# Four column-group chains for the compression products of a two-block transformer kernel, and a padded gather tile

## The reference, cut to what matters

```
hid = silu(einsum('td,edf->tef', t, w1)) * einsum('td,edf->tef', t, w3)
y = einsum('tef,efd->td', hid * combine[..., None], w2)
```

```
hid   = gelu((window + cmp_pe) @ cmp_w1[x])      # x = 0 keys, 1 values; 2048 -> 256
k_cmp, v_cmp = hid @ cmp_w2[x]                   # 256 -> 64
```

## Time and profile before

| | |
|---|---|
| median of three runs | 2472.61 us |
| the profiled execution: its time, its span | 2475.7 us, 2473.9 us |
| TensorE matmul busy | 2269.3 us, 92% of the span |
| VectorE, ScalarE, GpSimd busy | 837.0, 513.2, 53.9 us |
| mean granted TensorE clock | 0.953 of full speed |
| gather products L1320, 768 records | 149.4 us busy |
| compression products L2096, 128 records | 28.4 us busy |

### The profile page before, as it was taken

One profiled execution on the slowest core, in us unless ns is written; L12 is line 12 of the kernel. 1 busy time (PEld: TensorE's weight loads), 2 busy tenths in 40 slices (PEclk: granted clock), 3 DMA queues, 4 the chain that ended last, 5 costly groups with the idle time before them and its releaser, 6 DMA issues. The chain is left out here.

```text
span 2473.9 us, 33836 instructions
## 1 busy us (share of the span) xinstructions
PE 2269.3 (92%) x12870; PEld 1724.1 (70%) x12870; DVE 837.0 (34%) x1877; ACT 513.2 (21%) x1174; POOL 53.9 (2%) x28
## 2 busy tenths in 40 slices
PE   8998899886999889988699999999999999999999
PEld 6766766543876766544575777888877677788887
DVE  3465233232456324223335333211122532321112
ACT  2213320002312331000333422010012243201000
POOL 0120000000021000000000000000000000000000
PEclk9889889998988998999899999999999999999999
DMA  7220249996321063999654134333345403343433
GB/s 228 80 87 35 103 170 378 425 425 240 113 87 44 35 272 146 419 425 420 224 136 145 35 137 136 137 137 136 136 159 137 145 34 137 102 140 135 168 136 119
DMA packets 165171, 426.67 MB, mean 172 GB/s; under 512 B 40409, under 2 KB 54294, under 8 KB 140454
## 3 DMA queue, kind: packets, MB, share of 16 engines
q1 hardware_dynamic: 165030, 424.80, 46.6%
HBM read 419.06 MB, written 1.05 MB: 170 GB/s over the span
## 5 line engine op out<-in xcount | busy, mean ns | idle before, releaser
L2061 PE MATMUL bank<-hT,W 128*128 128x256 f32 (+1 forms) x1440 | 329.5, 385 | 6.9 <-ACT b_gates L2189 5.9
L2061 PEld LDWEIGHTS bank<-hT,W 128*128 128x128 f32 (+1 forms) x1440 | 269.4, 190 | 53.0 <-issue 12.3
L261 PE MATMUL bank<-hT,W 128*128 128x272 f32 x928 | 247.6, 427 | 16.8 <-issue 11.7
L261 PEld LDWEIGHTS bank<-hT,W 128*128 128x128 f32 x928 | 191.3, 209 | 65.9 <-issue 23.3
L3038 PE MATMUL bank<-hT,W 128*128 128x256 f32 x1024 | 225.5, 381 | 6.7 <-DVEq L3095 6.7
L3054 PE MATMUL bank<-u_hid,W 128*128 128x256 f32 x1024 | 223.3, 379 | 0.0
L3038 PEld LDWEIGHTS bank<-hT,W 128*128 128x128 f32 x1024 | 195.6, 191 | 34.3 <-issue 7.4
L3054 PEld LDWEIGHTS bank<-u_hid,W 128*128 128x128 f32 x1024 | 194.6, 190 | 26.5
L1320 PE MATMUL bank<-e_sel,rowsH 128*128 128x128 f32 (+1 forms) x768 | 149.4, 328 | 0.0
L1434 PE MATMUL bank<-W,e_hs 128*32 128x256 f32 x1792 | 112.3, 409 | 32.3 <-DMA W<-in_w 29.8
L1320 PEld LDWEIGHTS bank<-e_sel,rowsH 128*128 128x128 f32 (+1 forms) x768 | 113.9, 204 | 37.2 <-issue 11.6
(11 more groups left out here) (555 smaller groups left out, 2784.4 us busy)
## 6 DMA issues: line engine op xcount, KB each, us to landing
W<-in_w SPq DMA_DIRECT2D x112, 1024.0 KB, 16.7
W<-in_w_in SPq DMA_DIRECT2D x41, 2048.0 KB, 8.1
e_Wd<-in_w SPq DMA_DIRECT2D x64, 1024.0 KB, 12.6
W<-in_w_up SPq DMA_DIRECT2D x16, 2048.0 KB, 8.4
W<-in_w_down SPq DMA_DIRECT2D x16, 2048.0 KB, 7.9
W<-in_w_out SPq DMA_DIRECT2D x8, 2048.0 KB, 8.2
e_w_ahead<-in_w SPq DMA_DIRECT2D x16, 1024.0 KB, 15.9
W<-in_mem_w_kv SPq DMA_DIRECT2D x6, 2048.0 KB, 10.3
```

The source lines that it names most:

```text
L261: mm = nc.tensor.matmul(bank[:, 0:T], w[:, k, c0:c0 + P], m.hT[:, k, :], **st)
L2061: mm = nc.tensor.matmul(o[0:n, 0:S2], w[:, k, a:a + n], m.hT[:, k, :], start=(k == 0), stop=(k == KT - 1))
```

## The change

**Gather.** `rowsH`'s first tile (16 tokens) is set to zero in all 128 rows by GpSimd at the start of `mix_and_route`; ScalarE waits for that before it copies the rows in; and the three products of a feature tile all take 128 rows.

**Compression.** The two chains of 16 become four chains of 8 in four column groups (keys first half, keys second half, values first half, values second half), issued alternately into partitions 0, 32, 64 and 96 of one bank, after both halves of `win` are ready. `win` has 32 columns, of which the last two are set to zero. VectorE copies the 128 x 256 result to `hid`; two products with a constant 0/1 matrix `halves` (128 x 64) sum the halves and turn them at once (`hidT`), and VectorE copies that out. The gelu runs on 128 x 128 numbers, already turned, so the four transposes and ScalarE's copy go; the factor 0.5 moves into later copies. The list of projections is now `vs` 0, `cmp`, `vs` 1, `hidT`, `gv` 0.

```diff
@@ gpsimd, mix_and_route
+                nc.gpsimd.memset(m.rowsH[:, 0, :], 0.0)
+                pool.drain().then_inc(S["r_padded"], 1)
@@ scalar, mix_and_route
+                act.wait_ge(S["r_padded"], 1)
@@ gather
-        for c, (t0, nt) in enumerate(TILES):
-            mm = nc.tensor.matmul(o, m.rowsH[0:nt, c, d * P:(d + 1) * P], m.sel[0:nt, c, :], start=(c == 0), stop=(c == 2))
+        for c in range(3):
+            mm = nc.tensor.matmul(o, m.rowsH[:, c, d * P:(d + 1) * P], m.sel[:, c, :], start=(c == 0), stop=(c == 2))
@@ constants2
+    u = np.arange(64)
+    c["halves"] = (i[:, None] // 64 == u[None, :] // 32) & (i[:, None] % 32 == u[None, :] % 32)
@@ Products
-        for j in range(2):
-            add(("vs", j), 2.0, "act")
-        for x in range(2):
-            add(("cmp", x), 5.5, "dve")
+        add(("vs", 0), 2.0, "act")
+        add("cmp", 10.0, "dve")
+        add(("vs", 1), 2.0, "act")
+        add("hidT", 1.0, "dve")
@@ products, tensor
-        for c in range(2):
-            yield F.start(("vs", c))
-            by_token(("vs", c), c, w, 3 * P, P)
-        for x in range(2):
-            yield F.start(("cmp", x))
-            w = weights(f"cmp{x}", 16)
-            pe.wait_ge(S["h_win"], x + 1)
-            o = taken(pe, ("cmp", x))
-            for k in range(16):
-                mm = nc.tensor.matmul(o[0:2 * N_CMP, 0:256], m.win[:, x, k, :], w[:, k, :], start=(k == 0), stop=(k == 15))
-            mm.then_inc(S["f_mm"], 1)
+        yield F.start(("vs", 0))
+        by_token(("vs", 0), 0, w, 3 * P, P)
+        yield F.start("cmp")
+        w_cmp1 = [weights(f"cmp{x}", 16) for x in range(2)]
+        pe.wait_ge(S["h_win"], 2)
+        o = taken(pe, "cmp")
+        for k in range(8):
+            for q in range(4):
+                x, i = q // 2, 8 * (q % 2) + k
+                mm = nc.tensor.matmul(o[32 * q:32 * q + 32, 0:256], m.win[:, x, i, :], w_cmp1[x][:, i, :], start=(k == 0), stop=(k == 7))
+        mm.then_inc(S["f_mm"], 1)
+        yield F.start(("vs", 1))
+        by_token(("vs", 1), 1, w, 3 * P, P)
+        yield F.start("hidT")
+        pe.wait_ge(*F.made(S, "cmp"))
+        o = taken(pe, "hidT")
+        for e in range(2):
+            mm = nc.tensor.matmul(o[:, 64 * e:64 * e + 64], m.hid[:, e * P:(e + 1) * P], m.halves[:, :], start=True, stop=True)
+        mm.then_inc(S["f_mm"], 1)
@@ products, vector
+        yield F.end("cmp")
+        dve.wait_ge(S["f_mm"], done("cmp"))
+        nc.vector.tensor_copy(m.hid[:, :], bank("cmp")[:, 0:256]).then_inc(S["f_dve"], 1)
+        yield F.end("hidT")
+        dve.wait_ge(S["f_mm"], done("hidT"))
+        nc.vector.tensor_copy(m.hidT[:, 0, :], bank("hidT")[:, 0:P]).then_inc(S["f_dve"], 1)
@@ heads2, tensor and scalar: the transposes and the copy go
-                mm = nc.tensor.transpose(B[0][:, (2 * x + e) * 32:(2 * x + e) * 32 + NC2], gl[:, x, e * P:(e + 1) * P], m.ident[0:NC2, 0:NC2])
-        nc.scalar.activation(hidT, B[0][:, 0:128].rearrange("p (x e n) -> p x e n", x=2, e=2)[:, :, :, 0:NC2], ACT.Copy, scale=0.5)
@@ heads2, vector
+        yield F.end("vc") + 3.5
+        nc.vector.memset(m.win[:, :, :, 2 * N_CMP:32], 0.0)
...
+        nc.vector.tensor_tensor(gl, m.hidT[:, 0, :], m.hidT[:, 0, :], ALU.mult)
+        nc.vector.tensor_scalar(gl, gl, 0.044715, 1.0, ALU.mult, ALU.add)
+        nc.vector.tensor_tensor(gl, gl, m.hidT[:, 0, :], ALU.mult)
...
+        nc.vector.scalar_tensor_tensor(m.hidT[:, 1, :], gl, 1.0, m.hidT[:, 0, :], ALU.add, ALU.mult)
```

More of the change, by code:

```diff
@@ L1632 @@
 s_idx s_rel s_acc s_logit s_logit_sb s_max s_exp s_den s_prob s_pT s_pT_sb s_pv s_out
-o_mm o_added n1_centred n1_mean n1_squares n1_var n1_rstd n1_scaled n1_done r_logitT r_logitT_sb r_logit r_exp_in r_exp r_masks r_rows r_rows_sb r_counts r_ranks r_nb r_starts r_ended r_spread r_token_row r_table
+o_mm o_added n1_centred n1_mean n1_squares n1_var n1_rstd n1_scaled n1_done r_logitT r_logitT_sb r_logit r_exp_in r_exp r_masks r_rows r_rows_sb r_counts r_ranks r_nb r_starts r_ended r_spread r_token_row r_table r_padded
 e_w1_ahead e_w1_in e_w3_in e_down_in
@@ L1992, in products @@
     MOST = (0, 1)
-    last = {"kv0": ("mk", 3), "kv1": ("mv", 1), "nkw": ("vwg", 1), "gqk": ("gqk", 3), "q": ("q", 3), "nkv": ("vs", 1), "cmp0": ("cmp", 0), "cmp1": ("cmp", 1),
+    last = {"kv0": ("mk", 3), "kv1": ("mv", 1), "nkw": ("vwg", 1), "gqk": ("gqk", 3), "q": ("q", 3), "nkv": ("vs", 1), "cmp0": "cmp", "cmp1": "cmp",
             "gv": ("gv", 1), "gr": ("gr", 3), "mq": ("mq", 3), "br1": ("branch", 1, 7), "br2": ("branch", 2, 7), "br0": ("branch", 0, 7), "wo0": ("wo", 3), "wo1": ("wo", 7)}
@@ L2299, in heads2 @@
     m.kk = take(2, 2, S2)
[L2300 to L2304, removed]
+    m.win = take(2, 16, 32)
+    kq = take(5, N_CMP)
+    m.hid = take(1, 256)[:, 0, :]
+    m.hidT = take(2, P)
+    gl = take(1, P)[:, 0, :]
+    hidT = m.hidT[:, 1, :].rearrange("p (e x n) -> p x e n", e=2, x=2)
     B = ps[2:5]
@@ L2321, in on_tensor @@
         mm.then_inc(S["h_rope"], 1)
[L2322 to L2326, removed]
-                mm = nc.tensor.transpose(B[0][:, (2 * x + e) * 32:(2 * x + e) * 32 + NC2], gl[:, x, e * P:(e + 1) * P], m.ident[0:NC2, 0:NC2])
-        mm.then_inc(S["h_turn"], 1)
         yield max(C + 9, H + 22)
         pe.wait_ge(S["small_loaded"], 48)
+        pe.wait_ge(S["h_qk"], 1)
         pe.wait_ge(S["h_hidT"], 1)
@@ L2363, in on_scalar @@
         act.wait_ge(S["h_gin"], 1)
-        nc.scalar.activation(gl[:, :, :], gl[:, :, :], ACT.Tanh, scale=0.7978845608028654)
+        nc.scalar.activation(gl, gl, ACT.Tanh, scale=0.7978845608028654)
         act.drain().then_inc(S["h_gexp"], 1)
-        yield max(C + 8, H + 21.5)
-        act.wait_ge(S["h_turn"], 1)
-        nc.scalar.activation(hidT, B[0][:, 0:128].rearrange("p (x e n) -> p x e n", x=2, e=2)[:, :, :, 0:NC2], ACT.Copy, scale=0.5)
-        act.drain().then_inc(S["h_hidT"], 1)
         yield max(C + 10.5, H + 23.5)
         act.wait_ge(S["h_comp"], 1)
-        nc.scalar.activation(kq[:, 0, :], B[1][:, 0:N_CMP], ACT.Copy)
-        nc.scalar.activation(kq[:, 1, :], B[1][:, 0:N_CMP], ACT.Square)
+        nc.scalar.activation(kq[:, 0, :], B[1][:, 0:N_CMP], ACT.Copy, scale=0.5)
+        nc.scalar.activation(kq[:, 1, :], B[1][:, 0:N_CMP], ACT.Square, scale=0.5)
         act.drain().then_inc(S["h_ksq"], 1)
@@ L2410, in on_vector @@
         yield max(C + 1, H + 20)
[L2411 removed]
         dve.drain()
[L2413 removed]
+        nc.vector.tensor_tensor(gl, m.hidT[:, 0, :], m.hidT[:, 0, :], ALU.mult)
         dve.drain()
[L2415 removed]
+        nc.vector.tensor_scalar(gl, gl, 0.044715, 1.0, ALU.mult, ALU.add)
+        dve.drain()
+        nc.vector.tensor_tensor(gl, gl, m.hidT[:, 0, :], ALU.mult)
         dve.drain().then_inc(S["h_gin"], 1)
@@ L2418, in on_vector @@
         dve.wait_ge(S["h_gexp"], 1)
-        nc.vector.scalar_tensor_tensor(gl[:, :, :], gl[:, :, :], 1.0, m.hid[:, :, :], ALU.add, ALU.mult)
-        dve.drain().then_inc(S["h_gelu"], 1)
+        nc.vector.scalar_tensor_tensor(m.hidT[:, 1, :], gl, 1.0, m.hidT[:, 0, :], ALU.add, ALU.mult)
+        dve.drain().then_inc(S["h_hidT"], 1)
         yield max(C + 11, H + 24)
         dve.wait_ge(S["h_comp"], 1)
-        nc.vector.tensor_copy(m.vcmp[:, :], B[2][0:N_CMP, 0:P])
+        nc.vector.tensor_scalar(m.vcmp[:, :], B[2][0:N_CMP, 0:P], 0.5, None, ALU.mult)
         dve.drain().then_inc(S["h_vcmp"], 1)
@@ L3127 @@
 SEMS2 = """params_turned t_angles t_tables small_loaded p_sq p_ms p_rstd p_done f_mm f_act f_dve
-h_kk h_sq h_ms h_win h_xs h_rope h_qk h_gelu h_turn h_hidT h_comp h_vcmp h_ksq h_kms h_kxs h_krope h_kcmp h_rs h_gin h_gexp h_krs
+h_kk h_sq h_ms h_win h_xs h_rope h_qk h_hidT h_comp h_vcmp h_ksq h_kms h_kxs h_krope h_kcmp h_rs h_gin h_gexp h_krs
 n_pT_sb n_clogit n_bias n_logit0 n_logit1 n_prob n_pcT n_pT n_pcT_sb n_out n_pv n_gexp n_max n_exp
@@ L3150, in second_block @@
         m.rot, m.causal_bias, m.cmp_mask, m.cmp_bias = K["rot"], K["causal_bias"], K["cmp_mask"], K["cmp_bias"]
-        m.inv_freq, m.sums, m.pairs = K["inv_freq"], K["sums"], K["pairs"]
+        m.inv_freq, m.sums, m.pairs, m.halves = K["inv_freq"], K["sums"], K["pairs"], K["halves"]
         m.ones = sb("ones2", [1, P])
```

## The result

The kernel after takes 2442.73 us (median of four runs, 2431.89 to 2443.39) where four runs of the kernel before on the same chip take 2472.6 (2469.65 to 2474.36): a ratio of 0.987, interval 0.984 to 0.990. Forecast were 2439, range 2430 to 2454. The profiled execution took 2442.4 us with a span of 2440.6; the sum had said 2442.4 for it, from 2475.7 before.

What follows compares the result with a forecast made beforehand. TensorE was taken to bound the kernel except where expert transfers or VectorE's and ScalarE's chain do. 22.8 - 2.0 + 12.8 - 0.3 = 33.3 us off 2475.7 gave 2442.4 profiled, 2439 as median; range 2430 to 2454.

Steps and rivals of the forecast that it cites:

- Which stage bounds what: Experts: TensorE bounds the first stage, transfers the second; only a layer's first two gathers count, later ones are hidden.
- The gather: First two gathers of each layer, padded: 5.4 us per 48 records at full clock; transfers start 11.4 us earlier a layer.
- the better rival: Clock returns after 3 us in the gather and stays up in the compression: 42 us off, 2431; chance 0.13.
- The choice for an early return of the clock: First gather, padded: full clock returns about 6 us after its start, so the gather ends 6.7 us earlier.
- the rival in which it stays low: Clock stays low through the first gathers, leaving 5.6 us a layer there: 2451 in all; chance 0.17.
- the 1.0 at the layer's end: End of each layer's experts: 1.0 us lost as TensorE stands longer before the last w3 and low clock is likelier.
- The compression's replay: Second block, from cmp to gv 1: shorter chains less new waits put gv 1 6.4 us earlier a layer.
- The clock's cancelling: Compression: 2.5 us regained at gv 1 and low clock after the new waits cancel; between -4 and +2.5 a layer.
- The table: Loading the constant `halves` in the block of constants costs 0.3 us, once (0 to 1).
- Padding worth nothing: Rival: padding gives nothing where it counts, or transfers start no earlier; only the compression's 12.5 us left, 2460; chance 0.08.
- New waits that bring the clock down: Rival: the compression's new waits lower the clock in both layers, 3.4 us more each: 2446; chance 0.13.
- The slower rival: Clock stays at 0.50 from cmp on after the new waits; with 60 us of it, 27 us slower, 2500; chance 0.03.

Runs made afterwards that it cites:

- windows first: Kernel after, with VectorE preparing `win` ahead of the gated unit's reduce and ScalarE's squares planned 3 us earlier: 2428.91 us, ratio 0.983 to the kernel before.
- the four heights: Kernel before, with the first of the three products of a feature tile taking 16, 32, 64 and 128 rows in turn: 2461.06 us, one run.

## Why the prediction was right, step by step

**Which stage bounds what** held. That only the first two gathers count is shown by the kernel that pads only these; that the transfers follow by the issues 8.1 and 11.1 us earlier (8.5 and 11.4 forecast) and the same GB/s. The loads of the first issue were just through as the next came at 383.38 (the DMA share from 383.4 to 384.0 is 0.07); they had been reckoned through 1.1 us ahead of it.

**The gather** held. Start to start 5.4 us for 48 at full clock, by 368.64 and the next product 5.36 later; the clock back by 354, 6.2 us after the gather began ("about 6"), the up products 7.11 ("7.0"). In the second layer it was at 1.00 by 931, 3 us after the start, as the better rival had it. The zeroing was over 47 us before ScalarE's first copy of rows (290.1 and 337.3), so it cost nothing. The choice for an early return of the clock decided: the rival in which it stays low (2451) lost in all twenty padded layers. By that rival's sum the changes of rows by themselves are worth 5.6 us a layer of the 11.1, so about half of the gain before the transfers is the clock's, an estimate. The stage gives 10.1 us a layer on the mean of the ten padded profiles (229.4 against 239.5), forecast 10.4 with the 1.0 at the layer's end.

**The compression's replay** held in its waits (2.81, 0.87, 2.39, 2.24 for 2.9, 0.75, 2.5, 2.05), and in the chains: at full clock, in the kernel with the windows first, 64 records take 3.66 us busy ("3.5" from start to start) in place of two times 7.03, 3.8 times less. In the profile after it is 5.25, as 3.2 us of it are at 0.50. The Trainium skill, "TensorE: Matmul & The Clock Gate", section "Measured speedup vs the span model", gives 2.38 times for three column tiles, and four in proportion would have been 4.4 us, an estimate; the runs do not agree with it, and the row of the same shape was the better guide.

**The clock's cancelling** was a lucky choice of a right mechanism. Low parts cost 1.6 us at cmp and 1.7 at gv 0, so gv 1 started 3.2 us later than the replay has it; then gv 1 gave back 2.5. In the profile after, the gain stood at 5.8 behind gv 1, forecast 6.4.

**Mis-sized** are two small terms. The mixers' stage gives 7.7 us a layer on the mean of the profiles (396.4 in five kernels with the old compression, 388.7 in four with that of the change), where 6.4 was forecast. The two layers of the first pair of profiles give 6.2 and 9.8; the second holds, in the profile before alone, 10 us more at the low level some 250 us into the layer, like the stretch shown above for the windows. Sorted by that stretch, the stage took 397.9 with it and 394.9 without before (five layers each), 390.4 (two) and 388.1 (six) with the new compression: 7.5 and 6.8 a layer. So about half of the 1.3 beyond the forecast is where such stretches fall, an estimate, and the other half is not accounted for; why they come in one profile and not in another stays open. The table costs some 0.5 by the means, forecast 0.3, and a scatter of 1.5 does not tell them apart. By stages the sum is 20.2 + 15.4 - 0.5 = 35 us. Medians gave 29.9 and 32.6; in the profile after the MLP's stages were 3.8 us longer than in the one before, in the same code, 232.99 and 235.68 us for 232.09 and 232.78, and in the profiles of other kernels they are at either level. That the profiled execution took just the 2442.4 of the sum is therefore luck: the experts gave 21.0 and the mixers 16.0 where 33.6 were forecast for both, the start of the program 1.5 more, and the MLP's 3.8 and a head of the second block 1.4 us longer took it back.

**The rivals.** Padding worth nothing (2460) fell with the gather alone and with the four heights. The Trainium skill, "TensorEngine Tiling (Array Packing)", section "When to Use Tiling", has a contraction of 32 rows as a case for four row tiles; that padding is then no gain was the prediction's conclusion, and for a lone low product between full ones the runs do not bear it out (8.51 us with 16 rows, 5.52 with 128). Small tiles beside one another were not run. New waits that bring the clock down (2446) came true in half: they do, in each layer (1.6 and 1.7 us, together the rival's 3.4), but gv 1 paid 2.5 back. The better rival's terms add up to 42.8, not 42, which puts it at 2430, at the edge of the range. The slower rival's long stretch at 0.50 appeared nowhere.

## What to carry to other kernels

Where products of unlike row counts alternate on TensorE, count the changes first: zero rows added to make them alike cost nothing here and saved a third of the gather's time at full clock. Small chains in different column groups overlapped here only when issued in turns of one product each, and the wait that gathering their inputs adds should be looked for in the order of the engine that makes them. Before valuing an edit in a stage bound by transfers, ask whether it comes before the transfers start; only there did it count.

## What was not expected of the hardware

- A change between 128 rows and 64 costs the same as between 128 and 16, about 0.2 us from start to start in place of 0.112, and it shows in two steps, into the new height and within it.
- A padded first gather brought the clock from 0.50 back to 1.00 within 7 us; with changes of rows between the same products it stayed at 0.50 for some 20 us in six layers of six, though TensorE was busy for 14.6 of 15 us of them.
- Stretches of 10 us at 0.50 come and go between profiles of like kernels in a part of the mixers where TensorE is busy 8.5 of 8.5 us. A layer's mixers are 2.3 to 5.8 us longer with one, as much as the edits of order that were to be measured.
